# Seven block products for eight in the query and key projection of a float32 block, with the norms set up beside the value projection

## The reference, cut to what matters

```python
proj = h @ w_in                                  # h 1024 x 1024, w_in 1024 x (3072 + 16)
q, k, v, f_pre = jnp.split(proj, [D, 2 * D, 3 * D], axis=-1)
q = rms_norm(q.reshape(B, S, N_HEADS, HEAD_DIM), q_g)     # 16 heads of 64
k = rms_norm(k.reshape(B, S, N_HEADS, HEAD_DIM), k_g)
log_f = jax.nn.log_sigmoid(f_pre + b_f)
F = jnp.cumsum(log_f, axis=1)
# then, in blocks of 128 queries: softmax(q.k * scale + F[t] - F[s]) over s <= t, times v
```

## Time and profile before

| What | Value |
|---|---|
| Median of 3 runs | 3110.76 us (3110.35 to 3114.27) |
| The profiled execution's own time | 3107.55 us |
| Its span | 3105.6 us |
| TensorE busy | 2885.3 us, 93% of the span |
| VectorE, ScalarE, GpSimd busy | 48%, 23%, 8% |
| Mean granted TensorE clock | 0.982 of full speed |
| DMA | 338.74 MB, 109 GB/s on average |

### The profile page before, as it was taken

One profiled execution on the slowest core, in us unless ns is written; L12 is line 12 of the kernel. 1 busy time (PEld: TensorE's weight loads), 2 busy tenths in 40 slices (PEclk: granted clock), 3 DMA queues, 4 the chain that ended last, 5 costly groups with the idle time before them and its releaser, 6 DMA issues. The chain is left out here.

```text
span 3105.6 us, 52287 instructions
## 1 busy us (share of the span) xinstructions
PE 2885.3 (93%) x20624; PEld 1881.2 (61%) x20624; DVE 1501.9 (48%) x4009; ACT 720.0 (23%) x1631; POOL 262.1 (8%) x343
## 2 busy tenths in 40 slices
PE   3999979999999999999999999999999797899996
PEld 2555546664588644886444777777777554444442
DVE  3222237773255556655564666666666457011115
ACT  2111135652210000000002344444343200111111
POOL 0000001100000000000000222222121100110101
PEclk9999989999999999999999999999999898899998
DMA  5011013321022454224444000000000110899975
GB/s 204 22 41 41 20 55 113 107 88 62 1 82 82 156 173 159 82 82 162 163 163 173 24 24 25 2 25 16 12 25 3 65 62 28 315 354 354 354 257 189
DMA packets 104151, 338.74 MB, mean 109 GB/s; under 512 B 6896, under 2 KB 16624, under 8 KB 94592
## 3 DMA queue, kind: packets, MB, share of 16 engines
q1 hardware_dynamic: 95984, 306.35, 27.6%
q0 software_dynamic: 6912, 25.17, 2.1%
q10 hardware_dynamic: 1040, 4.19, 0.3%
HBM read 302.60 MB, written 33.10 MB: 108 GB/s over the span
## 5 line engine op out<-in xcount | busy, mean ns | idle before, releaser
L293 PE MATMUL qkv_pq<-qkv_wq,h_hT 128*128 128x384 f32 x1024 | 330.5, 486 | 0.0
L1672 PE MATMUL rwkv_ps<-all_main,pre_ws 128*128 128x256 f32 x1152 | 290.9, 389 | 0.0
L293 PEld LDWEIGHTS qkv_pq<-qkv_wq,h_hT 128*128 128x128 f32 x1024 | 194.5, 190 | 136.2 <-issue 0.9
L1015 PE MATMUL mlp_ps<-mlp_w2s,all_main 128*128 128x512 f32 x512 | 239.6, 592 | 0.0
L2593 PE MATMUL ex_pg<-all_main,ex_xT 128*128 128x512 f32 x512 | 225.7, 594 | 0.0
L1672 PEld LDWEIGHTS rwkv_ps<-all_main,pre_ws 128*128 128x128 f32 x1152 | 207.7, 190 | 28.8
L2039 DVE TENSOR_TENSOR all_tail<-rwkv_ps,all_tail 128x256 f32<-128x256 f32 x216 | 91.6, 424 | 191.2 <-PE rwkv_ps L1778 144.5
L1015 PE MATMUL mlp_ps<-all_main 128*128 128x512 f32 x384 | 183.2, 593 | 0.7 <-DVE all_main L1228 0.7
L2593 PEld LDWEIGHTS ex_pg<-all_main,ex_xT 128*128 128x128 f32 x512 | 97.6, 191 | 122.5 <-issue 122.5
L1015 PEld LDWEIGHTS mlp_ps<-mlp_w2s,all_main 128*128 128x128 f32 x512 | 96.6, 190 | 117.8 <-issue 105.1
L1983 POOL TENSOR_TENSOR all_tail<-all_tail,pre_cst 128x256 f32<-128x256 f32 x120 | 100.0, 849 | 472.7 <-DVE all_tail L2039 299.2
(11 more groups left out here) (415 smaller groups left out, 4783.9 us busy)
## 6 DMA issues: line engine op xcount, KB each, us to landing
mlp_w2s<-in_w SPq DMA_DIRECT2D x64, 1024.0 KB, 5.0
all_main<-in_w_gu SPq DMA_DIRECT2D x32, 2048.0 KB, 8.9
all_early<-in_w SPq DMA_DIRECT2D x32, 1024.0 KB, 4.9
att_wa<-in_w_ada SPq DMA_DIRECT2D x32, 512.0 KB, 3.9
all_early<-in_w_d SPq DMA_DIRECT2D x16, 1024.0 KB, 10.5
all_main<-in_w_d SPq DMA_DIRECT2D x16, 1024.0 KB, 10.8
y_rows<-ex_y SPq DMA_DIRECT2D x32, 512.0 KB, 3.1
qkv_wq<-in_w_qkv SPq DMA_DIRECT2D x8, 1536.0 KB, 6.6
```

What stands on the lines that cost most here:

```text
L293: last = nc.tensor.matmul(pq[:, b, 0:QN], lhsT=hT[:, k, t * P:(t + 1) * P], rhs=wq[:, n, k, :], start=(k == 0), stop=(k == KT - 1))
L1015: last = nc.tensor.matmul(ps[:, PRODUCTS.index(name), :], lhsT=lhsT, rhs=rhs, start=j == 0, stop=j == FPAIRS - 1)
L1672: last = nc.tensor.matmul(ps[:, bank, 0:UT], lhsT=ws[:, n, k, :], rhs=xT[:, k, (col + NB) % S:(col + NB) % S + UT], start=(k == 0), stop=( ...
```

## The change

Queries and keys (chunks 0 to 3 of 512 columns) are computed by Strassen's scheme in Winograd's form. The tokens are cut into two halves, the 1024 input features into two halves, and a chunk's columns into two halves of 256. A unit (c, i) is a chunk and one pair of token tiles, i and i + 4: seven products of 4 x 256 columns make the four output blocks of that pair. There are 16 units. Values (chunks 4 and 5) are computed plainly, 8 products of 512 columns for each token tile.

- **Token sums** S1, S2, S4 are made once, 12 VectorE operations of 128x512, into the part of `main` where the values will be; S3 takes the place of the block A21 in `hT` and is turned back into A21 after the last unit.
- **Column sums** T1, T2, T4 are made once a chunk, and T3 in place of B12 in the weight buffer: 4 VectorE operations of 128x1024. Those of chunk c + 1 stand in VectorE's stream behind the last unit of chunk c.
- **In each unit** ScalarE copies the first product out of PSUM; VectorE does 7 additions of 128x256, each with one operand in PSUM; ScalarE squares the four output blocks, in one buffer `sq`, and VectorE sums each.
- The gate chain is cut into steps that stand between the first units; its products use PSUM banks 6 and 7.
- The hardware loop is gone: all instructions are written out. Eight PSUM banks are used in turn.
- Set-up of the norms (mean, root, reciprocal, gains) and `stage(0)` of GpSimd move behind the units, beside the values' products. Their copies out of PSUM are shared by VectorE (even tiles) and ScalarE (odd tiles). Values are not squared any more.
- `norm` and `gain` move to the program's scope, and the second program's `par_all` uses the memory of `norm`. Some small tiles of the second program are allocated later.

```diff
+    PRODUCTS = ("m1", "m2", "m5", "m6", "m7", "m4", "m3")
+    LAST_PAIR = ("m5", "m6", "m4", "m1", "m2", "m7", "m3")
...
@@ sync
-                with sp.Fori(1, CH // 2) as i:
-                    for n in range(2):
-                        sp.wait_ge(mm, (2 * i + n - 1) * TT)
-                        sp.dma_start(wq[:, n, :, :], w_qkv[2 * i + n]).then_inc(w_in[n], 16)
+                for h in range(2):
+                    sp.dma_start(gain[h * HD:(h + 1) * HD, 0:2], qk_gain).then_inc(gain_in, 16)
...
+                for c in range(2, CHUNKS):
+                    if c - 2 < SEVENTHS:
+                        sp.wait_ge(mm, 28 * (c - 1))
+                    sp.dma_start(wq[:, c % 2, :, :], w_qkv[c]).then_inc(w_in[c % 2], 16)
@@ tensor
+                def product(c, i, name):
+                    at = mm_at[c, i, name] - 1
+                    if at >= 8:
+                        before = steps[at - 8]
+                        if before[2] == "m1":
+                            pe.wait_ge(taken, 4 * before[0] + before[1] + 1)
+                        else:
+                            pe.wait_ge(part, max(part_at(before[0], before[1], r) for r in READS[before[2]]))
...
+                    if name in ("m5", "m6", "m3", "m7"):
+                        pe.wait_ge(tokens, ("m5", "m6", "m3", "m7").index(name) + 1)
+                    if name in ("m5", "m6", "m7", "m4"):
+                        pe.wait_ge(columns, 4 * c + ("m5", "m6", "m7", "m4").index(name) + 1)
...
+                    for k in range(HK):
+                        last = nc.tensor.matmul(ps[:, bank_of[c, i, name], 0:HN], lhsT=weights(k), rhs=moving(k),
+                                                start=k == 0, stop=k == HK - 1)
+                    last.then_inc(mm, 1)
...
+                for c in range(SEVENTHS, CHUNKS):
+                    pe.wait_ge(w_in[c % 2], 16 * (c // 2 + 1))
+                    for t in range(TT):
+                        m = (c - SEVENTHS) * TT + t
...
+                        for k in range(KT):
+                            last = nc.tensor.matmul(ps[:, m % 8, :], lhsT=hT[:, k, t * P:(t + 1) * P], rhs=wq[:, c % 2, k, :],
+                                                    start=(k == 0), stop=(k == KT - 1))
@@ scalar
+                for c in range(SEVENTHS):
+                    for i in range(4):
+                        first(c, i)
+                        for name in SQUARES:
+                            squares(c, i, name)
...
+                act.wait_ge(prep, 1)
+                nc.scalar.activation(norm, norm, ACT.Sqrt).then_inc(root, 1)
+                for m in range(1, 2 * TT, 2):
...
+                    nc.scalar.copy(main[:, t, c * QN:(c + 1) * QN], ps[:, m % 8, :]).then_inc(v_taken_a, 1)
@@ vector
+                def gather(c, i):
+                    dve.wait_ge(taken, 4 * c + i + 1)
+                    add(c, i, "c11", block_of(c, i, "c11"), "m2", first_copy)
+                    add(c, i, "u2", u2, "m6", first_copy)
+                    dve.wait_ge(part, part_at(c, i, "u2"))
+                    reduce_squares(c, i, "c11")
+                    add(c, i, "u3", u3, "m7", u2)
+                    add(c, i, "u4", u2, "m5", u2)
+                    dve.wait_ge(part, part_at(c, i, "u3"))
+                    add(c, i, "c22", block_of(c, i, "c22"), "m5", u3)
+                    add(c, i, "c21", block_of(c, i, "c21"), "m4", u3)
+                    reduce_squares(c, i, "c22")
+                    reduce_squares(c, i, "c21")
+                    dve.wait_ge(part, part_at(c, i, "u4"))
+                    add(c, i, "c12", block_of(c, i, "c12"), "m3", u2)
+                    reduce_squares(c, i, "c12")
...
+                for c in range(SEVENTHS):
+                    if c == 2:
+                        dve.wait_ge(f_out, 16)
+                    for i in range(4):
+                        gather(c, i)
+                        next(gates_step, None)
+                    if c + 1 < SEVENTHS:
+                        for n in range(4):
+                            column_sum(c + 1, n)
+                for k in range(HK):
+                    last = tt(A21[k], A11[k], A21[k], ALU.subtract)
+                last.then_inc(restored, 1)
...
@@ gpsimd
+                pool.wait_ge(set_up, 3)
+                for w in range(2):
+                    q = main[:, :, w * D:w * D + P].rearrange("p t (h d) -> p t h d", d=HD)
+                    nc.gpsimd.tensor_tensor(q, q, norm[:, :, w * HEADS:w * HEADS + 2].unsqueeze(3).to_broadcast([P, TT, 2, HD]),
+                                            ALU.mult).then_inc(staged, 1)
@@ stage_attention: the set-up, the gain's DMAs and stage(0) are taken out; TensorE
                 def turn_qk(p, r):
-                    if r == 0:
-                        pe.wait_ge(staged, 2 * p + 2)
+                    if r == 0 and p:
+                        pe.wait_ge(staged, 2 * p)
```

More of the change, by code:

```diff
@@ L22 @@
 QKV = 3 * D
-QN = 384
 D_FF = 4 * D
@@ L244, in _, with stage_qkv @@
                         last.then_inc(turned, 1)
-def stage_qkv(nc, hT, w_qkv, w_f, b_f, qkv, ss, f_rows, work):
-    CH = QKV // QN
-    HPC = QN // HD
+QN = 512
+def stage_qkv(nc, hT, w_qkv, w_f, b_f, qk_gain, main, ss, f_rows, gates, norm, gain):
+    CHUNKS = QKV // QN
+    SEVENTHS = 4
+    HK, HN = KT // 2, QN // 2
+    HPB = HN // HD
+    PRODUCTS = ("m1", "m2", "m5", "m6", "m7", "m4", "m3")
+    LAST_PAIR = ("m5", "m6", "m4", "m1", "m2", "m7", "m3")
+    PARTS = ("c11", "u2", "u3", "u4", "c22", "c21", "c12")
+    READS = {"m1": (), "m2": ("c11",), "m6": ("u2",), "m7": ("u3",), "m5": ("u4", "c22"), "m4": ("c21",), "m3": ("c12",)}
+    BLOCKS_OF = {"c11": (0, 0), "c22": (1, 1), "c21": (1, 0), "c12": (0, 1)}
+    SQUARES = ("c11", "c22", "c21", "c12")
     with Scope(nc, "qkv") as s:
@@ L297, in _, with squares @@
             @block.scalar
             def _(act):
[L299 to L310, removed]
+                def squares(c, i, name):
+                    n = square_at(c, i, name)
+                    if n >= 2:
+                        act.wait_ge(summed, n - 1)
+                    act.wait_ge(part, part_at(c, i, name))
+                    t2, n2 = BLOCKS_OF[name]
+                    at = c * QN + n2 * HN
+                    nc.scalar.activation(sq, main[:, i + 4 * t2, at:at + HN], ACT.Square).then_inc(squared, 1)
@@ new lines, in first @@
+                def first(c, i):
+                    act.wait_ge(mm, mm_at[c, i, "m1"])
+                    if c or i:
+                        before = (4 * c + i - 1) // 4, (4 * c + i - 1) % 4
+                        act.wait_ge(part, part_at(before[0], before[1], "u2"))
+                    nc.scalar.copy(first_copy, ps[:, bank_of[c, i, "m1"], 0:HN]).then_inc(taken, 1)
+                for c in range(SEVENTHS):
[3 more added lines that the diff above has]
+                            squares(c, i, name)
+                        if c == 0 and i == 0:
+                            act.wait_ge(f_lin, 3)
+                            nc.scalar.activation(fe, fe, ACT.Exp).then_inc(f_act, 1)
+                            act.wait_ge(f_act, 1)
+                            nc.scalar.activation(fe, fe, ACT.Ln, bias=1.0).then_inc(f_act, 1)
@@ new lines, in gather @@
+                def gather(c, i):
[14 more added lines that the diff above has]
+                    reduce_squares(c, i, "c12")
+                    dve.wait_ge(part, part_at(c, i, "c12"))
@@ L423, in stage_attention @@
         f_in = [s.sem("f_in0"), s.sem("f_in1")]
[L424 removed]
+        staged = s.sem("staged")
         scored = [s.sem("scored0"), s.sem("scored1")]
@@ L442, in _ @@
             def _(sp):
-                for h in range(2):
-                    sp.dma_start(gain[h * HD:(h + 1) * HD, 0:2], qk_gain).then_inc(gain_in, 16)
                 for p in range(HEAD_PAIRS + 2):
```

220 lines of the change are left out of this document (145 added, 75 removed).

## The result

The changed kernel takes 3071.64 us (median of 4 runs, 3069.66 to 3075.22), the kernel before 3110.56 us beside it (4 runs, 3108.92 to 3114.27). The ratio is 0.9871, 95% interval 0.9858 to 0.9883: 36 to 44 us less. Two later sets of the same kernel gave 0.9879 (0.9857 to 0.9901) and 0.9881 (0.9864 to 0.9897). From profiled execution to profiled execution the time went from 3107.55 to 3072.45 us, 35.1 us less.

What follows compares the result with a forecast made beforehand. The prediction took TensorE's column count to bound the projection and the set-up chain to bound the handover to attention. Its terms, -27.4 + 3.5 - 12.0 = -35.9 us, took the median from 3110.76 to 3075 us, range 3066 to 3090.

Steps and rivals of the forecast that it cites:

- Columns: Projection loop: 330.5 us of TensorE records replaced by 193.2 for queries and keys plus 109.9 for values, -27.4 us.
- Chunk changes: Projection: VectorE's block additions hidden inside units, TensorE stalling 1.15 us at each of three chunk changes, +3.5 us.
- the chain after m7: Chunk's last unit: additions, squares and sums after m7 run nearly in series before the first column sum, about 4.9 us.
- Start of the stage: Projection start: token sums, column sums, A21's replacement and gate steps all finish before their users, 0 us.
- Handover: Projection to attention: set-up hidden beside values' products gives 9.7 us, faster clock the rest, -12.0 us.
- The part that the clock was to give: Handover: clock stays at 2.4 GHz, saving 1.8 us in four transpose rounds and 0.5 to 1 us in first scores.
- the prediction's own list: Signs of a wrong forecast: 256-column records over 216 ns apart, bank waits inside units, clock 0.50 in first transposes, longer attention.
- the edits with one answer: Written-out loop, values' squares and sums dropped, moved memory tiles: 0 each, the last within 0.5 us either way.
- `frow` just hidden: Attention start: loads land 4.9 to 6.8 us after issue, first row maximum needs them about 7 us into the stage.
- The rival of exposed loads: The 896 records of 256 columns: fully exposed weight loads cost 190 ns each, 170 us, total 3245; chance 0.05.
- The weaker handover: Handover gives only its waits, clock low or `frow` late: -9.7 us for -12, total 3077 to 3079; chance 0.16.
- VectorE did not set the pace: Rival denied here: VectorE's chain sets units at 14 us, not 12.1, giving back 30 us, total 3105; chance 0.03.

Runs made afterwards that it cites:

- plain_qk: Changed kernel with queries and keys back to eight plain products of 512 columns, norm set-up still beside the values' products: 3102.45 us, ratio 0.9966 to the kernel before.
- double_sums: Changed kernel with each unit's four sums of squares made twice on VectorE: 3080.62 us, ratio 0.9901 to the kernel before.
- cols_early: Changed kernel with the next chunk's column sums ahead of the chunk's last unit in VectorE's stream: 3071.64 us, ratio 0.9874 to the kernel before.
- warm: Changed kernel plus unread filler products behind the last values' product and each of four transpose rounds: 3069.43 us, ratio 0.9869 to the kernel before.
- setup_late: Changed kernel with the norm set-up and first pair's scaling back at the start of attention, seven products kept: 3087.29 us, ratio 0.9921 to the kernel before.
- early_turn: cols_early with the first pair's four rounds of transposes and copies also moved beside the values' products: 3069.55 us, ratio 0.9877 to the kernel before.
- best_fill: early_turn plus unread filler products, one behind the last values' product and seven behind the first scores: 3071.36 us, ratio 0.988 to the kernel before.
- v128: Changed kernel with the values' products in four pieces of 128 columns, 1024 records for 256: 3077.96 us, ratio 0.9893 to the kernel before.
- after_third: The changed kernel repeated without any edit, as the base beside best_fill: 3072.95 us.

## Why the prediction was right

**Columns (-27.4 forecast).** Right: 25.2 us net in the trace. With the three chunk changes added back, 0.6 us each, 27.0 are the columns'. plain_qk confirms it within a microsecond (24.4 us net). The spacings taken from another stage of the program held within half a nanosecond (110.0 us / 256 = 429.7 ns; 16 records in 3.45 us, 215.6 ns).

**Chunk changes (+3.5).** Right place and cause (double_sums, cols_early), size off: 1.8 us. The step that failed is the chain after m7, 4.9 us in my sum. In the trace it runs from 132.27 us, VectorE's first addition behind m7, to 136.43 us, the column sum: 4.16 us.

```profile
132.27 0.76 DVE L437 TENSOR_TENSOR qkv_small<-qkv_ps,qkv_small 128x256 f32<-128x256 f32 x2 [0.20 <-PE qkv_ps L334]
132.94 0.75 DVE L437 TENSOR_TENSOR all_main<-qkv_ps,qkv_small 128x256 f32<-128x256 f32 x2
133.45 0.42 ACT L377 ACTIVATE all_gates<-all_main 128x256 f32<-128x256 f32 x1 [1.90 <-DVE all_main L437]
...
133.90 0.42 DVE L443 TENSOR_REDUCE all_gates<-all_gates 128x4 f32<-128x256 f32 x1 [0.21 <-ACT all_gates L377]
```

I added the durations of rows, but VectorE's operations begin 0.33 to 0.35 us apart where they follow each other, while their rows last 0.42. And I put 0.15 us on each handover from engine to engine, where a square's row ends at 133.87 and its sum begins at 133.90. So the column sum began 14.7 us after the unit's start and not 15.4.

**Start of the stage (0).** Right: the column sums were done 4 us earlier than my bound, and no product of the first units waits.

**Handover (-12.0).** 11.0 measured. The part up to the first transpose, 9.7 in my sum, is 9.85. The part that the clock was to give, 2.3, is 1.2: the step that failed is "with a gap of 1.3 us I take it to stay up". The gap was as short as forecast, but the clock fell in the third round, after some 4 us in which TensorE worked about half of the time; with fillers it stayed (warm, 1.8 us more). By the prediction's own list, a clock at 0.50 in the first transposes was a sign that the forecast is wrong: it was at 1.00 in the first two rounds and at 0.50 in the fourth. The first row maximum came 9.5 us after the last copy began, where 8 to 9 us after the last product were named. A sentence among the edits with one answer was wrong too: the values' squares and sums, put at 0, are 1.4 us of the 9.85 (setup_late), though the sum had them through the stage's start. "`frow` just hidden" held: the row maximum came 8.5 us after the load's issue, and could have started 4.2 us (early_turn) to 5.6 us (best_fill) after it.

**Weight loads.** The rival of exposed loads was wrong: the 896 records stand 215.6 ns apart. So was its basis, that 25.6 ns are left between a load's 190 and the next record (v128).

**Rivals.** The weaker handover described the clock correctly and was given 0.16. VectorE did not set the pace. Total: 35.1 us by profiles, medians of three sets 38.9, 34.0 and 37.3 less, for 35.9 forecast. The sum came out closer than its terms, and that part is luck: the chunk changes cost 1.7 us less than forecast, the handover gave 1.0 less, the columns 0.4 less, and 1.3 us (later start, rest of the span) had no term. Nor can one pair of profiles carry a match within a microsecond: by the medians the change is worth 34 to 39 us, and three profiles of the changed kernel alone differ by 6 us.

## What to carry to other kernels

Cost a chain on one engine by the distance between starts, not by the rows' durations, and the same for weight loads: look for a place in the trace where such records follow each other. When set-up work is moved out of a gap between stages, what is left of the gap may keep TensorE busy only half of the time, and here its clock fell in it although no idle time was as long as 2 us; ask next which load is issued only at the stage's start. Differences of 2 to 3 us in a total that scatters by up to 11 are read inside one profile, between two marks that lie around the edit.

## What the runs showed of the hardware that was not expected

Loads with rows of 192 ns follow each other 111.8 ns apart (v128). The granted clock fell to 0.50 in a handover in which TensorE was never idle for as long as 2 us (the windows above), while in early_turn it was still at 1.00 through 394 to 396 us, in which TensorE did nothing, and fell in the busier microseconds behind it.

One and the same program has stretches of 3 to 7 us at the lower level that come and go from one execution to the next. At 690, 2407 and 3025 us of after_third TensorE had been idle for 1.8 to 2.1 us just before; the first profile has a gap as long or longer in each of these places, and its clock stayed up. At 755 us the clock falls in all three profiles of the changed kernel, and TensorE's row has no gap there. What stands ahead of the fall, in the first profile, are 32 products of a single column:

```profile
748.41 3.63 PE L161 MATMUL mlp_ps<-all_ones,all_tail 128*128 128x1 f32 x32
```

So a busy share near 100% does not tell that the clock will stay up. The coming and going of these stretches makes the whole difference of 6 us between two profiles of this kernel.
